# Second block of a two-block model: decay sums made beside the input product, the linear heads' outputs kept by token with norm and gate inside their own stage, and the two softmax maps of a differential head subtracted in one VectorE pass

## The reference, cut to what matters

```
u = rms_norm(h, norm_mix);  z = u @ w_in       # split: gq gk gv gg ga dq dk dv
# linear heads: 4 heads, keys of 64, values of 128, 16 chunks of 64 tokens
log_a = log_sigmoid(ga @ w_a_up + b_a) / 16
b = cumsum(log_a within a chunk);  eb, enb = exp(b), exp(-b)
a = where(tri, (q*eb) (k*enb)^T, (q*enb) (k*eb)^T)           # within a chunk
o = a @ v + (q*eb) @ S_n                                       # S_n: state before chunk n
S_{n+1} = exp(b_last) * S_n + (k*exp(b_last - b))^T v
o_gla = rms_norm(o per head, gla_norm) * silu(gg)
# differential heads: 4 heads, two maps of keys of 64, values of 128, causal by chunk
w = softmax(s0) - lam * softmax(s1)
o_diff = rms_norm(w @ v per head, diff_norm) * (1 - lam_init)
h = h + concat(o_gla, o_diff) @ w_out                          # then conv FFN, gated embedding, norm
```

## Time and profile before

| | |
|---|---|
| median of 3 runs | 4898.54 (4897.96 to 4912.95) |
| profiled execution | 4914.21, its span 4912.4 |
| mean granted TensorE clock | 0.90 |
| stages touched | about 3200 to 3871 in the span |

### The profile page before, as it was taken

One profiled execution on the slowest core, in us unless ns is written; L12 is line 12 of the kernel. 1 busy time (PEld: TensorE's weight loads), 2 busy tenths in 40 slices (PEclk: granted clock), 3 DMA queues, 4 the chain that ended last, 5 costly groups with the idle time before them and its releaser, 6 DMA issues. The chain is left out here.

```text
span 4912.4 us, 57286 instructions
## 1 busy us (share of the span) xinstructions
PE 4367.7 (89%) x22438; PEld 3424.3 (70%) x22438; DVE 2386.5 (49%) x3810; ACT 1206.5 (25%) x2099; POOL 434.7 (9%) x579
## 2 busy tenths in 40 slices
PE   6989799877999889979996799799698599998997
PEld 4888488665777678747874688587555368887875
DVE  2477688533111256667854100482435545554344
ACT  3234233221111132423322111311134221111232
POOL 1000000100222110000010111100023110000011
PEclk8999899886999989999996899899557799999998
DMA  7100000126777431000020888212000121112111
GB/s 310 45 18 1 19 1 1 65 100 276 248 248 248 150 148 35 1 18 2 1 78 36 324 326 300 68 48 78 2 1 1 60 71 47 47 47 77 48 60 52
DMA packets 75264, 454.45 MB, mean 93 GB/s; under 512 B 9889, under 2 KB 13745, under 8 KB 59057
## 3 DMA queue, kind: packets, MB, share of 16 engines
q1 hardware_dynamic: 60928, 400.21, 21.6%
q0 software_dynamic: 13088, 47.19, 3.5%
q10 hardware_dynamic: 1040, 4.19, 0.2%
HBM read 395.99 MB, written 55.57 MB: 92 GB/s over the span
## 5 line engine op out<-in xcount | busy, mean ns | idle before, releaser
L2214 PEld LDWEIGHTS psum<-words,words 128*128 128x128 f32 x4096 | 514.2, 192 | 16.2 <-issue 16.2
L2214 PE MATMUL psum<-words,words 128*128 128x160 f32 (+1 forms) x4096 | 515.4, 289 | 1.4 <-DVE words L428 0.9
L711 PE MATMUL psum<-words,words 128*128 128x512 f32 x1104 | 442.0, 400 | 24.6 <-DVE words L749 20.2
L713 PE MATMUL psum<-words,words 128*128 128x512 f32 x1104 | 438.6, 397 | 0.0
L712 PE MATMUL psum<-words,words 128*128 128x512 f32 x1104 | 438.3, 397 | 0.0
L2284 DVE TENSOR_TENSOR words<-words,psum 128x160 f32<-128x160 f32 (+1 forms) x128 | 38.9, 304 | 635.2 <-ACT words L2262 635.2
L1067 PEld LDWEIGHTS psum<-words 128*128 128x128 f32 x1968 | 268.2, 193 | 94.4 <-issue 78.7
L1684 PE MATMUL psum<-words,words 128*128 128x428 f32 (+1 forms) x720 | 254.0, 353 | 25.9 <-DVE words L1777 25.9
L1496 PE MATMUL psum<-words 96*128 96x512 f32 (+1 forms) x600 | 266.4, 529 | 7.5 <-POOL words L1494 7.5
L1067 PE MATMUL psum<-words 128*128 128x128 f32 x1968 | 271.1, 276 | 0.4 <-DVE words L1189 0.4
L711 PEld LDWEIGHTS psum<-words,words 128*128 128x128 f32 x1104 | 209.5, 190 | 75.9 <-DVE words L749 21.5
(11 more groups left out here) (379 smaller groups left out, 8183.5 us busy)
## 6 DMA issues: line engine op xcount, KB each, us to landing
words<-in_w_gate SPq DMA_DIRECT2D x32, 2048.0 KB, 7.7
words<-in_w_up SPq DMA_DIRECT2D x32, 2048.0 KB, 12.1
words<-in_w_down SPq DMA_DIRECT2D x32, 2048.0 KB, 11.4
words<-in_ada_w SPq DMA_DIRECT2D x24, 2048.0 KB, 16.1
words<-in_w_in SPq DMA_DIRECT2D x55, 512.0 KB, 3.4
words<-in_w_up SPq DMA_DIRECT2D x44, 512.0 KB, 3.5
words<-in_w_down SPq DMA_DIRECT2D x44, 256.0 KB, 2.6
words<-in_x SPq DMA_DIRECT2D x2, 5120.0 KB, 22.1
```

The costliest lines, as they stand in the source:

```text
L711: pe.matmul(out, hi[:, j, w], S.parts[0](kt, t0, nt), start=(kt == 0), stop=False)
L713: mm = pe.matmul(out, lo[:, j, w], S.parts[0](kt, t0, nt), start=False, stop=(kt == KD - 1))
L2214: mm = pe.matmul(k.bank[m % 2][:, u * W:(u + 1) * W], ring[:, j, w0:w0 + P], xgT[:, j, kt, 0:W], start=(kt == 0), stop=(kt == KD - 1))
```

## The change

- **Decay sums in `project2`.** The stage `decays` is removed. At n = 17 SyncE waits for `sent` and then loads `w_a_up` and `keep`. After tile 18 (`DECAY`) TensorE does the four 16-row products into banks 4 to 7; ScalarE adds the bias; VectorE and ScalarE do the log-sigmoid and the scan at n = 18, 19 and 20, between evictions.
- **Linear stage.** The exponentials and the products with q and k are now at its head, in halves of 1024 columns; one of them (`kb`) is on GpSimd, which also multiplies the gates by `gla_norm`. State steps 2t + 1 and 2t + 2 are done inside step t, ahead of the scores of t + 1. The outputs are made by token: the attention tile and the 64 x 64 pieces of q are the weights, v and the state the moving side (128 columns). They go to one pair of banks. ScalarE copies them out and squares them with a sum per token and head; mean, root and inverse are over 16 elements, twice; VectorE scales, TensorE transposes back, and VectorE multiplies by the gate on the way to `MIX`.
- **Attention.** `factors` makes -lam * sum0 / sum1, and `difference` does p1 * factor + p0 in one pass; map 0 is not divided by its sum. The sums of map 0 are kept, and the norm's epsilon is multiplied by their square. GpSimd's pass is gone.
- The stages `norm` and `gate_linear` of the linear heads are removed.

The core of the diff, with "..." for lines left out:

```diff
@@ project2
+    DECAY = 18
...
+        if n == DECAY:
+            for f in range(2):
+                dve.wait_ge(made["biased"], 2 * f + 2)
+                link(dve.scalar_tensor_tensor(eb[:, f, :], db[f], -1.0, db[f], ALU.mult, ALU.max))
+                ins = dve.tensor_scalar(db[f], db[f], 0.0, None, ALU.min)
...
+        if n == DECAY + 1:
+            dve.wait_ge(made["power"], 1)
+            dve.tensor_scalar(eb, eb, 1.0, None, ALU.add).then_inc(made["size"], 1)
+        if n == DECAY + 2:
+            dve.wait_ge(made["logged"], 1)
+            dve.wait_ge(made["fetched"], 32)
+            for f in range(2):
+                link(dve.tensor_tensor(db[f], db[f], eb[:, f, :], ALU.subtract))
+                link(dve.tensor_scalar(eb[:, f, :], db[f], 1.0 / 16.0, None, ALU.mult))
+                link(dve.tensor_tensor_scan(db[f], keep, eb[:, f, :], 0.0, ALU.mult, ALU.add))
...
+    def raw_decays(pe, n, S):
+        if n == DECAY:
+            pe.wait_ge(made["fetched"], 32)
+            for f in range(2):
+                for c in range(2):
+                    pe.matmul(k.bank[4 + 2 * f + c][:, :], wa[:, f * P:(f + 1) * P], PR[0:16, GA, 512 * c:512 * c + 512],
+                              start=True, stop=True).then_inc(made["raw"], 1)
...
     def park(sp, n, S, sent):
+        if n == FIRST:
+            sp.wait_ge(made["sent"], 16)
+            sp.dma_start(wa, k.a["w_a_up_2"]).then_inc(made["fetched"], 16)
+            sp.dma_start(keep, k.a["chunk_keep"]).then_inc(made["fetched"], 16)
@@ linear_attention, TensorE
+            def outs(t):
+                pe.wait_ge(aset, t + 1)
+                pe.wait_ge(s_ready, min(2 * t + 1, NCH - 1))
+                if t:
+                    pe.wait_ge(oout, 2 * t)
+                for f in range(2):
+                    for h in (2 * f, 2 * f + 1):
+                        pe.matmul(k.bank[4 + h % 2][:, f * P:(f + 1) * P], aT[:, t % 2, h * P:(h + 1) * P], V[:, t, h * P:(h + 1) * P],
+                                  start=True, stop=False, skip_group_check=True)
+                    for c in range(2):
+                        n = 2 * t + c
+                        for h in (2 * f, 2 * f + 1):
+                            if n:
+                                mm = pe.matmul(k.bank[4 + h % 2][64 * c:64 * c + 64, f * P:(f + 1) * P],
+                                               PR[row(h), GQ + f, n * GC:(n + 1) * GC], S[row(h), f, n, :],
+                                               start=False, stop=True, skip_group_check=True)
+                mm.then_inc(ofull, 1)
...
+            states(0)
+            pe.wait_ge(qs, 2)
+            pe.wait_ge(kbs, 2)
+            pe.wait_ge(qbs, 2)
+            pe.wait_ge(kks, 2)
             scores(0)
             for t in range(LT):
+                for n in (2 * t + 1, 2 * t + 2):
+                    if n < NCH - 1:
+                        states(n)
                 if t + 1 < LT:
                     scores(t + 1)
+                outs(t)
@@ linear_attention, GpSimd
+            for f in range(2):
+                pool.wait_ge(qbs, f + 1)
+                pool.tensor_tensor(kb[:, f, :], kb[:, f, :], kk[:, f, :], ALU.mult).then_inc(kbs, 1)
+            for h in range(GH):
+                pool.tensor_scalar(gate[:, h, :], gate[:, h, :], k.vec[:, k.v["gla_norm"] + h:k.v["gla_norm"] + h + 1], None,
+                                   ALU.mult).then_inc(grown, 1)
@@ differential_attention, VectorE
             def factors(n):
                 dve.wait_ge(ps, 2 * n + 2)
-                link(dve.reciprocal(s1[:, 3:4], s1[:, 2:3]))
-                dve.tensor_scalar(s1[:, 3:4], s1[:, 3:4], lam[:, 2:3], None, ALU.mult).then_inc(fs, 1)
-                link(dve.reciprocal(s0[:, 3:4], s0[:, 2:3]))
+                f = st[:, n % 3, 1, 3:4]
+                link(dve.reciprocal(f, sums(n, 1)))
+                link(dve.tensor_scalar(f, f, lam[:, 2:3], sums(n, 0), ALU.mult, ALU.mult))
...
             def difference(n):
                 i = units[n][1]
-                dve.wait_ge(w1, n + 1)
                 p0, p1 = (pr[:, n % 3, m, 0:(i + 1) * P] for m in range(2))
-                dve.scalar_tensor_tensor(p0, p0, st[:, n % 3, 0, 3:4], p1, ALU.mult, ALU.subtract).then_inc(w2, 1)
+                dve.scalar_tensor_tensor(p0, p1, st[:, n % 3, 1, 3:4], p0, ALU.mult, ALU.add).then_inc(w2, 1)
@@ second_block
     project2(k)
-    decays(k)
     linear_attention(k)
     differential_attention(k)
-    g = MIX[:, 0:GH, :]
-    norm(k, g, g, GH, LAT, vcol("gla_norm"), None, at_=XT0, width=P, each=True)
-    gate_linear(k)
```

More of the change, by code:

```diff
@@ L2387, in scaled @@
     def scaled(sem):
-        for name in ("done", "pos_in", "inv_in", "reduced", "trig", "put", "turned", "gates", "sent"):
+        for name in ("done", "pos_in", "inv_in", "reduced", "trig", "put", "turned", "gates", "sent", "fetched", "raw", "biased", "size", "power", "logged"):
             made[name] = sem()
@@ new lines, in root @@
+            def root(half):
+                act.wait_ge(meaned, half + 1)
+                m = ss[:, half * QUARTER:(half + 1) * QUARTER, :]
+                act.activation(m, m, ACT.Sqrt).then_inc(rooted, 1)
+            for f in range(2):
+                act.activation(kb[:, f, :], b[f], ACT.Exp, scale=-1.0).then_inc(falls, 1)
+            value(0)
+            value(1)
+            for f in range(2):
+                act.activation(eb[:, f, :], b[f], ACT.Exp).then_inc(rises, 1)
+            value(2)
@@ new lines, in _ @@
+            value(3)
+            for f in range(2):
+                act.wait_ge(tails, f + 1)
+                act.activation(kd[:, f, :], kd[:, f, :], ACT.Exp).then_inc(tailed, 1)
+            act.wait_ge(lasts, 2)
+            act.activation(dec[:, :], k.blast[:, :], ACT.Exp).then_inc(dec_set, 1)
+            for t in range(4, LT):
+                value(t)
+            for t in range(LT):
+                result(t)
+                if t == QUARTER:
+                    root(0)
+            root(1)
@@ L2622, in _, with state @@
             link = Links(dve, own)
-            dve.memset(aT, 0.0).then_inc(zer, 1)
-            for t in range(LT):
-                dve.wait_ge(vt, t + 1)
-                dve.tensor_copy(kdT[:, t, :], k.bank[2 + t % 2][:, 0:256]).then_inc(vt_d, 1)
-            dve.wait_ge(vt, LT)
-            link(dve.memset(S[:, :, 0, :], 0.0))
-            for n in range(NCH - 1):
+            def state(n):
                 dve.wait_ge(dsf, n + 1)
@@ new lines, in _ @@
+            for f in range(2):
+                dve.tensor_copy(last(f), by_chunk(b[f])[:, :, GC - 1:GC]).then_inc(lasts, 1)
+            for f in range(2):
+                dve.wait_ge(lasts, f + 1)
+                dve.tensor_tensor(by_chunk(kd[:, f, :]), last(f).to_broadcast([P, NCH, GC]), by_chunk(b[f]), ALU.subtract).then_inc(tails, 1)
+            for f in range(2):
+                dve.wait_ge(falls, f + 1)
+                dve.scalar_tensor_tensor(qb[:, f, :], q[:, f, :], 0.125, kb[:, f, :], ALU.mult, ALU.mult).then_inc(qbs, 1)
@@ new lines, in _ @@
+            for f in range(2):
+                dve.wait_ge(kbs, f + 1)
+                dve.wait_ge(kds, f + 1)
+                dve.tensor_tensor(kk[:, f, :], kk[:, f, :], eb[:, f, :], ALU.mult).then_inc(kks, 1)
+            dve.wait_ge(vt, LT)
+            link(dve.memset(S[:, :, 0, :], 0.0))
+            dve.wait_ge(dec_set, 1)
+            dve.wait_ge(ld, 32)
+            dve.wait_ge(zer, 1)
+            state(0)
+            masked(0)
+            for t in range(LT):
+                for n in (2 * t + 1, 2 * t + 2):
+                    if n < NCH - 1:
+                        state(n)
+                if t + 1 < LT:
+                    masked(t + 1)
+                if t == QUARTER:
+                    mean(0)
+                if t == QUARTER + 1:
+                    inverse(0)
+                if t > QUARTER + 1:
+                    scale(2 * (t - QUARTER - 2))
+                    scale(2 * (t - QUARTER - 2) + 1)
@@ L2655, in differential_attention @@
+            mean(1)
+            inverse(1)
+            for t in range(4):
+                scale(4 + t)
+                place(t)
+            for t in range(4, LT):
+                place(t)
 def differential_attention(k):
@@ L2921, in _ @@
                 place(DH - 1, q, N - 1)
-def gate_linear(k):
-    PR, MIX = k.at(PR0, NPROJ, NLAT), k.at(HT0, KD, NT)
-    with k.stage() as (block, sem):
-        @block.vector
-        def _(dve):
-            for h in range(GH):
-                o = MIX[:, h, NCTX:NT]
-                dve.tensor_tensor(o, o, PR[:, GG + h, :], ALU.mult)
 def feed_up(k):
```

255 lines of the change are left out of this document (129 added, 126 removed).

## The result

| | before | after |
|---|---|---|
| median, us | 4903.85 (4 runs, 4897.96 to 4912.95) | 4792.55 (4 runs, 4788.0 to 4802.84) |
| profiled execution, us | 4914.21 | 4794.33 |
| its span, us | 4912.4 | 4792.2 |

The ratio is 0.9774, with a 95% interval of 0.975 to 0.9799: 111 us less by the medians. The time forecast was 4794.

The account below looks back on a forecast made before the run. Bound: VectorE-ScalarE chains in the removed stages, TensorE mostly at 1.2 GHz in linear stage and attention. Terms -45.9 + 6 - 7.6 - 5 - 51.8 = -104.3 us gave profile 4810, median 4794; range 4766 to 4818.

Parts of the forecast that it names:

- What bounds the kernel: Two stretches: `decays` and norm plus `gate_linear` end by a VectorE-ScalarE chain; linear stage and attention keep TensorE busy, mostly at 1.2 GHz.
- Input product, +6: Input product takes over the front half of `decays`: thin products 3.5, clock 1, tile 18 stall 1.5; together +6 us.
- the "1" for the clock: In the input product: 1 us added in case the thin 16-row products pull the clock down, bounds 0 to 3.5.
- Prelude, 21.3: Head of the linear stage: 19.2 us, plus 2.1 for one VectorE product slowed by GpSimd; bounds 19.2 and 29.7.
- The loop, 50: Linear stage's loop: 61 us at 1.2 GHz (7.8 a step), 38 at 2.4 GHz (4.7); half at either level, 50.
- The argument against 2.4 GHz: Against the linear loop running at 2.4 GHz throughout: state products of a 64 x 64 tile ran at 0.50 in the profile.
- Never leaves 1.2 GHz: Rival: the linear loop stays at 1.2 GHz, 61 us instead of 50, total 4805; chance 0.20.
- serialised: Rival: in the linear loop TensorE waits for mask and copies, 11.4 us a step, +41, total 4835; chance 0.08.
- 2.4 GHz throughout, or four at a time: Rival: linear loop at 2.4 GHz or products four at a time, attention catches more; 12 + 10 less, 4772; chance 0.17.
- Tail, 12: End of the linear stage: last squares, mean, root, inverse, then scaling and placement, 12 us, bounds 9 to 16.
- Attention, -5: Attention without GpSimd's pass: end wait of 2.31 goes, 2 off waits for ScalarE's copy; -5 us, bounds 0 and -19.
- Norm and gate, -51.8: The linear heads' norm and `gate_linear` stages go, their work covered by idle engines in the linear loop: -51.8 us.

## Why the prediction was right, and where not

- *What bounds the kernel.* Right. The two stages with an idle TensorE went with their full 97.7 us. Put back, the front half of the one took 27.3 and the other 52.0, and what lies behind the attention grew by no more than 1.1.
- *Input product, +6.* 8.9 in the profile. The stall of tile 18 was read rightly from SyncE's order (0.7 to 2.0 in nine profiles, 1.5 forecast). The evictions came late and cost nothing: TensorE waits for none. Mis-sized was the "1" for the clock: a fall costs 3 and comes in four of nine executions, so that the stage grows by 5 to 7 without a fall and by 8 to 10 with one.
- *Prelude, 21.3.* 21.2 measured, by luck in its parts. One product was to be slowed by 2.1; in fact three were, by 1.2, 0.8 and 0.8.
- *The loop, 50.* The step that failed. "I take half the loop at either level" was a choice between 61 and 38, and the loop took 32.2. Two parts of it: the level was 1.00 from 3469.2 on, in the outputs of the first of the eight steps, and the 4.7 a step at that level was too much by 1.1. VectorE does not set the step (busy 2.8 us of each 3.63, and TensorE waits for it in none), which is 0.8 of the 1.1. The rest is in TensorE's own 3.9, which were 3.63, and there three errors partly cancel. The outputs' state products took 0.66 for 0.85, as they go four at a time. The scores took 1.09 for 0.85. And two state steps took 0.60 for 0.9, since the 0.9 each of before was a chain with VectorE and not TensorE's work: mostly at 0.50, twelve of them took 10.74 us there, 1.79 for two (line below), and the first two of the new loop, at 0.50 too, took 1.07. The argument against 2.4 GHz rested on rows at 0.50 of state products alone. In the kernel with states first they again stand alone at 0.50, and the loop behind them is at 1.00 all the same, so those rows said nothing of the loop. In the Trainium skill, TensorEngine Tiling (Array Packing), Key Properties, says that tiles work independently; the trace agrees, eight records in the time of four.

```profile
3490.08 10.74 PE L2570 MATMUL psum<-words,words 64*64 64x128 f32 x96 [0.44 <-DVE words L2635]
```

- *The rivals and the signs.* "Never leaves 1.2 GHz" and "serialised" are out: one wait of 0.9 for ScalarE's copy in the last step is all, though by the letter even that is a sign that the forecast had named for being wrong. The steps were to be 7.8 or 4.7 and were 3.63, and from the input product to the attention there were to be 83 us and were 63.7: these signs say that the linear stage was forecast wrongly, whatever the total. "2.4 GHz throughout, or four at a time" was the right mechanism for the loop, both halves of it, and it was given 0.17. Its total of 4772 was not met, since the attention didn't catch more and the base of 4898.5 was low. That the time came out within 1.5 is luck: a loop 18 too dear stood against a base 5 to 10 too low, an input product 2.9 too cheap and the distance between single profiles and medians.
- *Tail, 12.* 10.3. *Attention, -5.* -6.2 here, 4 to 7 at an equal clock; the part put to ScalarE's wait is not there. *Norm and gate, -51.8.* Right to the tenth, which is the length of two stages that were cut, and the squares in the loop were free.

## What to carry to other kernels

Stages in which TensorE idles are worth their whole length if their work fits beside a stage that TensorE bounds; check the order of the DMA queue and the granted clock at the new place, since that is where the small loss was (1.2 and 3 us here). Issue products of small tiles so that neighbours lie in different quarters of the array: here that saved 1.1 us of 4.7 a step at the same clock, and with operands and states as before it decided between the two clock levels. Where the clock is granted differently from run to run, compare a stage only with its granted clock beside it, and take the base from as many runs as the change. A total that is met says little of its terms: hold each stage against its own.

## What the runs showed of the hardware that was not expected

- A loop whose TensorE is called busy throughout runs at 0.50 (67.45 busy of 68.90) or at 1.00 for all but its first microseconds, after reordering of the same products alone (30.00 against 68.90 us, with operands and states the same).
- Beside four thin products of 16 rows in a row the clock fell for 6.8 us in four of nine executions of the same code; with two and two in none of three.
- Identical code of the attention took 241.2 to 259.8 us, mean granted clock 0.68 to 0.61, ten of eleven executions at 246.0 or less.
- GpSimd beside VectorE slowed one two-input pass of each pair and left the other at 1.21 us: to 2.05 and 2.06 beside GpSimd's passes of one input, to 2.41 beside one of two.
